# Search and choice of the sample queries' keys spread over 128 partitions, in two halves of each 32-partition group

## What is computed

```python
def indexer_topk(qi, wi, ki, q_pos, topk):
    s = einsum('bqhd,bld->bqhl', qi, ki) * IDX_DIM ** -0.5
    score = einsum('bqhl,bqh->bql', relu(s), wi) * N_IDX_HEADS ** -0.5
    score = where(key_pos <= q_pos, score, -inf)
    _, idx = top_k(score, topk)
...
q, k, v, qi, ki, wi, u = mixer_inputs(hs, pos_s, norm_mix_pre, w_in)      # 64 sample queries
ki_all = concatenate([cache_kidx[page_table], ki])                         # 4096 past + 8 new keys each
idx, valid = indexer_topk(qi, wi, ki_all, pos_s, 256)
a_o = sparse_attend(q, gathered keys, gathered values, valid)
y_ssm, hr, hi = s5_scan(...);  s_o = glu_out(y_ssm, w_glu, b_glu)
hs = residual_block(hs, a_o, s_o, w_out, ..., w_up, w_down, ...)           # the same for the prompt
```

## Time and profile before

| | before |
|---|---|
| median of 3 runs | 3765.61 us |
| lowest and highest run | 3762.29 and 3767.79 us |
| span of the profiled execution, first to last instruction | 3765.1 us |
| mean granted TensorE clock | 0.902 |
| busy share PE, DVE, ACT, POOL | 81%, 57%, 49%, 34% |

### The profile page before, as it was taken

One profiled execution on the slowest core, in us unless ns is written; L12 is line 12 of the kernel. 1 busy time (PEld: TensorE's weight loads), 2 busy tenths in 40 slices (PEclk: granted clock), 3 DMA queues, 4 the chain that ended last, 5 costly groups with the idle time before them and its releaser, 6 DMA issues.

```text
span 3765.1 us, 47305 instructions
## 1 busy us (share of the span) xinstructions
PE 3068.1 (81%) x15388; PEld 2414.3 (64%) x15388; DVE 2160.7 (57%) x4196; ACT 1845.4 (49%) x3065; POOL 1286.6 (34%) x1134
## 2 busy tenths in 40 slices
PE   7997535537778889997788999868888999789997
PEld 6886421214556668765577886546677888678885
DVE  4433952973356984467897443777995443643333
ACT  3322413722446755575674556756754554433333
POOL 1333510313013561252265114522663112235454
PEclk9998767767779999998899999989999999989998
DMA  4444344527332232123223112242222111522222
GB/s 153 141 138 166 64 153 108 135 68 222 99 113 76 81 94 68 55 78 136 97 77 95 54 43 63 81 148 69 72 90 83 54 40 50 177 81 87 79 79 76
DMA packets 201425, 361.56 MB, mean 96 GB/s; under 512 B 56202, under 2 KB 113612, under 8 KB 199740
## 3 DMA queue, kind: packets, MB, share of 16 engines
q1 hardware_dynamic: 182652, 332.01, 27.9%
q0 software_dynamic: 9312, 18.14, 1.5%
q10 hardware_dynamic: 9216, 8.39, 0.7%
HBM read 298.64 MB, written 67.01 MB: 97 GB/s over the span
## 4 chain that ended last, share of the span: by engine, by line
PE 42%; DVE 18%; issue 12%; ACT 5%; POOL 4%; DMA 2%; SPq 1%; ACTq 1%; POOLq 0%; DVEq 0%
PE r L1532 11%; PE r L1564 9%; PE po L1612 4%; PE r L1505 3%; PE tr L1603 3%; DVE junk_v_b L2242 3%; POOL acc_b L2008 2%; ACT junk_a_b L1873 2%; DVE trial_b L2194 2%; DVE up_b L2089 2%; DVE dn_b L2089 2%; PE sc L1580 1%; PE sc L1591 1%; PE sc L1590 1%; PE r L1675 1%
## 5 line engine op out<-in xcount | busy, mean ns | idle before, releaser
L1564 PE MATMUL r<-dn_b,h_b 128*128 128x512 f32 x2880 | 727.0, 408 | 111.8 <-DVE dn_b L2089 51.2
L1564 PEld LDWEIGHTS r<-dn_b,h_b 128*128 128x128 f32 x2880 | 551.4, 196 | 273.1 <-DVE dn_b L2089 61.7
L2008 POOL TENSOR_TENSOR acc_b<-acc_b,part_b 128x512 f32<-128x512 f32 x375 | 527.8, 1427 | 517.2 <-ACT part_b L1824 516.3
L1532 PE MATMUL r<-x_hi_b,up_b 128*128 128x512 f32 x2048 | 660.2, 396 | 7.6 <-DVE x_lo_b L2108 4.2
L1532 PEld LDWEIGHTS r<-x_hi_b,up_b 128*128 128x128 f32 x2048 | 389.2, 190 | 105.5 <-issue 13.0
L1873 ACT ACTIVATE junk_a_b<-score_b,trial_b 128x384 int8<-128x384 f32 (+13 forms) x266 | 347.4, 1306 | 148.5 <-DVE trial_b L2194 147.8
L1989 POOL TENSOR_TENSOR hr_b<-hr_b 128x512 f32<-128x512 f32 x128 | 153.5, 1199 | 738.4 <-ACT hr_b L1811 738.1
L1532 PE MATMUL r<-x_lo_b,up_b 128*128 128x512 f32 x1024 | 402.7, 393 | 0.0
L1824 ACT ACTIVATE part_b<-r 128x512 f32<-128x512 f32 x390 | 223.9, 594 | 225.0 <-PE r L1564 156.0
L1612 PEld LDWEIGHTS po<-V_sb,pT_b 128*128 128x128 f32 x2176 | 291.5, 195 | 23.2 <-issue 3.1
L1900 ACT ACTIVATE pT_b<-tr 128x512 f32<-128x512 f32 (+3 forms) x320 | 169.0, 528 | 259.5 <-PE tr L1603 257.8
(11 more groups left out here) (385 smaller groups left out, 5696.3 us busy)
## 6 DMA issues: line engine op xcount, KB each, us to landing
raw_b<-w_up SPq DMA_DIRECT2D x128, 512.0 KB, 3.8
raw_b<-w_down SPq DMA_DIRECT2D x128, 512.0 KB, 3.5
raw_b<-w_out SPq DMA_DIRECT2D x64, 256.0 KB, 3.2
kv_b<-kv_pages SPq DMA_DIRECT2D x96, 128.0 KB, 4.0
kv_b<-kv_pages POOLq DMA_DIRECT2D x96, 128.0 KB, 3.8
x_tok_sb<-x_all SPq DMA_DIRECT2D x17, 512.0 KB, 4.5
xT_sb<-xT_all SPq DMA_DIRECT2D x17, 512.0 KB, 4.8
kic<-kidx_d SPq DMA_DIRECT2D x4, 2048.0 KB, 8.5
```

The lines of the kernel that those rows point to most:

```text
L1532: mm = pe.matmul(x[:], wt[:, c], y[:, k], start=k == n == 0, stop=(k, n) == (KD - 1, 2))
L1564: mm = pe.matmul(x[:], f[:, tok], w[:, col], start=c == n == 0, stop=(c, n) == (KQ - 1, 2))
L2008: pool.tensor_tensor(dst, dst, part[:, add_no[key] % 2, :], ALU.add).then_inc(add_pool, 1)
```

## The change

The 64 queries no longer stand in 64 partitions with 4104 keys each. Each 32-partition group holds 16 queries twice: its first 16 partitions with the first 2048 past keys, its last 16 with the other 2048. Both have 8 columns for the new keys, 2056 in all; in the first half these are masked off.

The sums over the heads go to 128 rows (`wsel` has a zero-filled form for each half), two chunks of keys are accumulated in one bank, and one copy takes both. ScalarE counts columns 0 to 1095, VectorE 1096 to 2055. Wherever a count, or the number of ties in the other half, is needed, a `stream_shuffle` swaps the two halves of each group and an add joins them. `rep` gets one form for each half, so that one matmul of 128 rows by 128 columns takes the place of two of 64 by 64. The loads of `newmask` and `rep32` become 16 loads on POOL's queue.

```diff
-    CUT = 2064
+    HK = PAST // 2 + DECT
+    CUT = 1096
...
-        sjunk_a, sjunk = place_at("sjunk_a", [NS, CUT], BF16), place_at("sjunk", [NS, NK], BF16)
+        sjunk_a, sjunk = place_at("sjunk_a", [P, CUT], BF16), place_at("sjunk", [P, HK], BF16)
...
-                sp.dma_start(newmask[:], A["newmask"]).then_inc(ss_ld, 16)
...
-                sp.dma_start(rep32[:], A["rep"]).then_inc(ss_ld, 16)
...
-                        wait(pe, wt_ok, w)
+                        s = w % 2 if w < NC else 1
+                        wait(pe, wt_ok, w // 2 if w % 2 == 0 else 0)
                         for k in range(2):
-                            mm = pe.matmul(ring[2][0:NS, 0:m], wsel[:, k, :], rl[:, (2 * w + k) % 4, 0:m], start=k == 0, stop=k == 1)
+                            mm = pe.matmul(ring[2][:, 0:m], wsel[:, s, k, :], rl[:, (2 * w + k) % 4, 0:m],
+                                           start=k == 0 and w % 2 == 0, stop=k == 1 and s == 1)
...
-                    for b in range(2):
-                        mm = pe.matmul(x[64 * b:64 * b + 64, 0:m], rep[:, 2 * r + b, :], stie[:, c * KC:c * KC + m], start=False, stop=True)
-                    mm.then_inc(ss_full, 1)
+                    s = c // (NC // 2) if c < NC else 1
+                    at_ = c * KC - s * PAST // 2
+                    pe.matmul(x[:, 0:m], rep[:, s, 2 * r:2 * r + 2, :].rearrange("p b n -> p (b n)"), stie[:, at_:at_ + m],
+                              start=False, stop=True).then_inc(ss_full, 1)
...
+                    if u[0] == "SQ":
+                        for a in range(4):
+                            for z in range(2):
+                                rows, q = slice(32 * a + 16 * z, 32 * a + 16 * z + 16), slice(16 * a, 16 * a + 16)
+                                pool.dma_start(newmask[rows], A["newmask"][q]).then_inc(half_ld, 16)
+                                pool.dma_start(rep32[rows], A["rep"][q]).then_inc(half_ld, 16)
...
-                        pool.tensor_copy(rep[:], rep32[:]).then_inc(sprep, 1)
...
+                other_half = [*range(16, 32), *range(16)]
+
+                def whole(x, partner):
+
+                    c.step(dve.stream_shuffle(partner, x, other_half))
+                    c.step(dve.tensor_tensor(x, x, partner, ALU.add))
...
+                        whole(sboth[:, 0:1], sboth[:, 1:2])
...
-                    c.step(dve.tensor_scalar(sjunk[:, CUT:NK], smask[:, CUT:NK], strial[:].bitcast(F32), 0.0, ALU.is_ge, ALU.add,
+                    c.step(dve.tensor_scalar(sjunk[:, CUT:HK], smask[:, CUT:HK], strial[:].bitcast(F32), 0.0, ALU.is_ge, ALU.add,
...
                         c.step(dve.tensor_scalar(j, s, z(1), 0.0, ALU.is_ge, ALU.add, accum_out=z(2)))
+                        whole(z(2), z(6))
...
                         c.step(dve.tensor_scalar(e, s, z(3), 0.0, ALU.is_gt, ALU.add, accum_out=z(4)))
+                        whole(z(4), z(6))
...
+                        for n in range(2):
+                            c.up(dve.tensor_scalar(rep[:, n], rep32[:], second[:, n:n + 1], None, ALU.mult))
...
                         c.step(dve.tensor_tensor_scan(s, e, e, 0.0, ALU.add, ALU.bypass))
+                        c.step(dve.stream_shuffle(z(6), smask[:, HK - 1:HK], other_half))
+                        c.step(dve.tensor_tensor(z(6), z(6), second[:, 1:2], ALU.mult))
+                        c.step(dve.tensor_tensor(z(5), z(5), z(6), ALU.subtract))
...
-                        for k in range(2):
-                            dve.tensor_scalar(wsel[:, k, :], sel[:, k, :], wcol[:, k:k + 1], None, ALU.mult).then_inc(wsel_ok, 1)
+                        dve.memset(wsel[:], 0.0).then_inc(wsel_ok, 1)
+                        by_half = ident[:].rearrange("p (a z q) -> p z a q", a=4, z=2)
+                        c.step(dve.tensor_reduce(quads[:], by_half[:, 1], AX.X, ALU.add))
+                        c.step(dve.tensor_reduce(second[:, 1:2], quads[:], AX.X, ALU.add))
+                        c.step(dve.tensor_scalar(second[:, 0:1], second[:, 1:2], -1.0, 1.0, ALU.mult, ALU.add))
...
+                        for n in range(2):
+                            for k in range(2):
+                                dve.tensor_scalar(wsel[:, n, k].rearrange("p (a z q) -> p z a q", a=4, z=2)[:, n],
+                                                  sel[:, k].rearrange("p (a q) -> p a q", a=4), wcol[:, k:k + 1], None,
+                                                  ALU.mult).then_inc(wsel_ok, 1)
...
-                            dve.tensor_copy(smask[:, at_:at_ + m], ring[2][0:NS, 0:m]).then_inc(wt_ok, 1)
...
+                        elif w % 2:
+                            dve.wait_ge(wt_full, w + 1)
+                            dve.tensor_copy(smask[:, w // 2 * KC:w // 2 * KC + KC], ring[2][:, 0:KC]).then_inc(wt_ok, 1)
```

More of the change, by code:

```diff
@@ L1121, in blend @@
         at[0] = after_kv
-        smask = place_at("smask", [NS, NK], size=0)
+        smask = place_at("smask", [P, HK], size=0)
         sprob = place_at("sprob", [P, NK])
-        stie = place_at("stie", [NS, NK], BF16)
+        stie = place_at("stie", [P, HK], BF16)
         pTs = place_at("pTs", [P, 3, 4, P])
-        strial, sturn = place_at("strial", [NS, 1], I32), place_at("sturn", [NS, 1], I32)
-        scount, sboth, sbest = place_at("scount", [NS, 2]), place_at("sboth", [NS, 1]), place_at("sbest", [NS, 6])
+        strial, sturn = place_at("strial", [P, 1], I32), place_at("sturn", [P, 1], I32)
+        scount, sboth, sbest = place_at("scount", [P, 2]), place_at("sboth", [P, 2]), place_at("sbest", [P, 8])
+        second, quads = place_at("second", [P, 2]), place_at("quads", [P, 4])
         qid = place_at("qid", [NS, NIH, 2, HD])
         qiS = place_at("qiS", [P, DECB, NIH, DECT])
-        wcol, sel, wsel = place_at("wcol", [P, 2]), place_at("sel", [P, 2, NS]), place_at("wsel", [P, 2, NS])
-        newmask = place_at("newmask", [NS, DECT])
+        wcol, sel, wsel = place_at("wcol", [P, 2]), place_at("sel", [P, 2, NS]), place_at("wsel", [P, 2, 2, P])
+        newmask = place_at("newmask", [P, DECT])
         spt = place_at("spt", [1, DECB * NPAGE], I32)
         q16, qz = place_at("q16", [P, 4, P]), place_at("qz", [P, DECB, NKV, QPK, DECT])
-        rep32, rep = place_at("rep32", [NS, DECB, NS]), place_at("rep", [NS, DECB, NS], BF16)
+        rep32, rep = place_at("rep32", [P, DECB, NS]), place_at("rep", [P, 2, DECB, NS], BF16)
         vn = place_at("vn", [DECT, DECB, P])
@@ L1666, in sample_scores @@
                         pe.wait_ge(gate_ok, N_GATE)
-                        pe.wait_ge(sprep, 5)
+                        pe.wait_ge(sprep, 4)
                         pe.wait_ge(smask_ok, 1)
@@ L2059, in sample_part @@
                         pool.memset(aTs[:], 0.0).then_inc(sprep, 1)
[L2060 to L2062 removed]
+                        pool.wait_ge(ss_ld, 16 * (3 + DECB))
+                        pool.wait_ge(sprep, 2)
                         for n in range(NKV):
@@ L2294, in sample_search @@
                         dve.wait_ge(scount_ok, n)
-                        c.step(dve.scalar_tensor_tensor(out=sboth[:], in0=scount[:, 1:2], scalar=2.0, in1=scount[:, 0:1],
+                        c.step(dve.scalar_tensor_tensor(out=sboth[:, 0:1], in0=scount[:, 1:2], scalar=2.0, in1=scount[:, 0:1],
                                                         op0=ALU.mult, op1=ALU.subtract))
+                        whole(sboth[:, 0:1], sboth[:, 1:2])
                         back = -1.0 if b == BITS - 1 else float(2 ** b)
-                        c.step(dve.tensor_scalar(sturn[:], sboth[:], float(2 * TOPK - CUT), back, ALU.is_lt, ALU.mult))
+                        c.step(dve.tensor_scalar(sturn[:], sboth[:, 0:1], float(2 * TOPK - 2 * CUT), back, ALU.is_lt, ALU.mult))
                         if b == 0:
@@ L2341, in sample_part @@
                     elif u[0] == "SI" and 0 <= u[1] - 1 <= NC:
                         w = u[1] - 1
-                        m = KC if w < NC else DECT
-                        at_ = ((w % 2) * NC // 2 + w // 2) * KC if w < NC else PAST
-                        dve.wait_ge(wt_full, w + 1)
-                        if w < NC:
-                            dve.tensor_copy(smask[:, at_:at_ + m], ring[2][0:NS, 0:m]).then_inc(wt_ok, 1)
-                        else:
-                            dve.tensor_tensor(smask[:, at_:at_ + m], ring[2][0:NS, 0:m], newmask[:], ALU.add).then_inc(wt_ok, 1)
+                        if w == NC:
+                            dve.wait_ge(half_ld, 16 * 16)
+                            c.step(dve.tensor_scalar(quads[:, 0:1], second[:, 0:1], NEG, None, ALU.mult))
+                            c.step(dve.tensor_scalar(newmask[:], newmask[:], quads[:, 0:1], None, ALU.add))
+                            dve.wait_ge(wt_full, NC + 1)
+                            dve.tensor_tensor(smask[:, PAST // 2:HK], ring[2][:, 0:DECT], newmask[:], ALU.add).then_inc(wt_ok, 1)
+                        elif w % 2:
```

(2 more changed lines are left out.)

12 lines of the change are left out of this document (6 added, 6 removed).

## The result

The changed kernel takes 3731.36 us (median of 4 runs, 3730.24 to 3733.96) against 3766.70 us before (4 runs): ratio 0.9903, 95% interval 0.9891 to 0.9915. The profiled execution took 3730.24 us, with a span of 3728.6 us instead of 3765.1. On another chip the same kernel gave 3726.34 against 3773.32 us, 0.9882 [0.9865, 0.9898]. Two executions far outside all others, one of run 7 (4585 us) and one of the kernel before beside it (7054 us), are left out of what follows. The forecast was 3736.8 us: right in sign and inside its range, but 5.4 us above the measured median. Against the span it had summed 28.8 us of gain, and 36.5 us came.

A forecast was written before the change was run, and what follows sets the result against it. VectorE bounds the kernel from the late gates to the end of the choice. Gains of 0.2 + 3.3 + 10.0 + 12.3 + 3.0 = 28.8 us off the 3765.1 span, plus half a microsecond, gave 3736.8 us; range 3727 to 3750.

The forecast's parts named there:

- Start and SI: Work before gate 0: the start loses 0.4 us, SI gains 0.6, so gate 0 comes 0.2 us earlier.
- 128 weights instead of 64 cost nothing: In SI, the matmuls keep their 512 moving columns, so the wider weights add no time.
- POOL's issues cost nothing: At the start, POOL's 16 loads take 17.8 us and end near 565, before its next work at 573.09.
- Gates: Gates 9 to 15 speed up from 4.07 us each towards TensorE's 3.43, gaining 3.3 us.
- the choice between the ends: For gates 9 to 15, 3.3 us was taken from a range of 1.2 to 4.5 us gained.
- the collision: In gates 9 to 15, GpSimd's product holds up VectorE's settle, 3.9 us a gate, cutting the gain to 1.2 us.
- Counts and settles: Counts 16 to 31: shorter counts gain 18.0 us, exchanges cost 7.6, waits for ScalarE 0.4; 10.0 us gained.
- The slower rival: Each shuffle's load of lanes costs 1.28 us, like ScalarE's table load: 12 us slower, 3777.5 us; chance 0.04.
- Choice: Counts, marks, scan and last operations shrink from 4104 to 2056 columns, gaining 12.3 us (11.3 to 13).
- SS: The mask matmul saves time in 27 units of the first three rounds: 3 us gained, between 0 and 4.3.
- one bf16 matmul should be one such pass: 0.12 us less: In each SS unit, the single mask matmul takes one 0.214 us pass instead of 0.33 us for two.
- Rivals: Gates unchanged, exchanges dearer: 3744.6 us, 0.15; POOL slow: 3748, 0.07; lanes dear: 3777.5, 0.04; lost behind choice: 3765.6, 0.04.

The follow-up runs named there:

- run 7: Kernel before with one more count over 2040 columns ahead of the choice's first count; 3765.89 us, ratio 0.9991.
- run 8: Changed kernel with the 16 loads of newmask and rep32 issued by SP instead of POOL; 3735.11 us against 3726.34 for the changed kernel.
- run 2: Changed kernel with each exchange of the bits and of the choice's two counts done twice; 3747.63 us, ratio 0.9929.
- run 1: Changed kernel without the exchanges in the bits and the choice's two counts, each half searched by its own counts; 3723.50 us, ratio 0.9876.
- runs 3 and 9: Changed kernel with the mask added by two matmuls of 128 rows and 64 columns, 3730.47 us; changed kernel without any mask matmul, 3720.30 us.
- run 6: Changed kernel with the mask added by two matmuls of 64 rows and 64 columns, as in the kernel before; 3728.88 us, ratio 0.9908.
- run 4: Changed kernel with twelve more counts over 2056 columns before the choice's first count, 29 us late; 3759.85 us, ratio 0.9976.

## Why the prediction was right, and where it was not

*Start and SI* (forecast 0.2, measured 0.3): right in the sum by two errors that cancel. The start was to lose 0.4 us and gained 0.6 (the first bit of the prompt at 572.29 instead of 572.87): the first score came 1.6 us earlier, where I took 0.7, and `wsel` cost 1.0 on the path, where I took 1.1. SI was to gain 0.6 and lost 0.2: the 0.63 us of waiting before the last full chunk's sum went, but the step "128 weights instead of 64 cost nothing" failed, since a sum over the heads takes 1.98 us instead of 1.93 in each full chunk, and the last short one 0.58 instead of 0.37. That POOL's issues cost nothing held (0.49 us each; done at 556, forecast 565), and that SP's two issues count held (run 8).

*Gates* (3.3, measured 4.5): the floor. The step that missed is the choice between the ends: I let the collision begin behind some slack. It never set the pace: an operation held for 0.4 us in one bit of three fell among waits for ScalarE of 0.65 to 0.84 us. My bit had GpSimd's product end 3.24 us after a count starts; at 678 it ended 2.4 us after (679.00, count at 676.58), since the sigmoid stands ahead of ScalarE's next count and not behind it. Run 2 shows how near it is: 0.39 us a bit more brings it back, and then a single add is held for 1.06 us. The rule that I had set against the trace (the Trainium skill, SBUF — State Buffer, "Who interferes with whom": a VectorE operation with two SBUF inputs and a GpSimd one that reads SBUF exclude each other for a whole instruction) would have made this part 1.2 us. The trace agrees with the rule by the held adds, 1.06 us in run 2 and 0.31 at 710.60 in the changed kernel (which ends with GpSimd's product at 710.91), but its price came only with run 2's longer bits.

*Counts and settles* (10.0, measured 12.1): right in mechanism, mis-sized in its terms. The load of lanes is 0.01 us instead of 0.10 and the shuffle 0.15: an exchange costs 0.38 to 0.39 instead of 0.47 (run 1), 1.4 us over 16. VectorE's wait for ScalarE is 0.18 us in a bit without S unit, where I had 0.09. And behind gate 15 the settle of the prompt's bit (L2203, L2194 before) is no longer held in most bits (0.16 us at 717.20, where it has 0.34 at 726.12 in the kernel before), which I hadn't counted. On the instruction for the lanes (the Trainium skill, Vector Engine (DVE) Microarchitecture Reference, "The reshape front-end and per-opcode configuration") the trace agrees: it stands ahead of each shuffle, as LOAD_MASK_SELECT. The slower rival hung on its price and falls at 0.01 us.

*Choice* (12.3, measured 12.7): right, term by term (2.35, 1.28, 4.44 us).

*SS* (3.0, measured 8.2): wrong. The step "one bf16 matmul should be one such pass: 0.12 us less" failed: two 64-column matmuls run side by side and cost what one costs, and both shapes, 64 rows or 128 columns, pay for a change of tiling (runs 3 and 9). What was gained there instead goes with granted clock: 4.1 us by the shape of the mask's matmuls (run 6); most of the other 4.1 us in the first and third stretch (2.2 and 1.7 between the two sets of rows), which go in part with where the stage falls (2.7 us lost in run 4, 1.8 gained in run 7) and in part with something that no run isolated. I had written that the last round and what follows gains nothing; 4.6 us were gained in those two stretches.

*Rivals.* None came true. The gates left their old rate and the exchanges were cheaper than forecast, POOL's loads were done 16 us before its next work, and the lanes cost 0.01 us. The gain was not lost behind the choice: 6.9 us more came than stood at the first SS matmul. Of the 7.7 us by which the sum fell short of the span, 5.2 lie in the SS rounds; there the mechanism was wrong, and that a gain came at all in that part is luck.

## What to carry to other kernels

Rows that fill half of the partitions can be split into halves of their columns. An exchange of one number between partitions of a group costs 0.38 us by shuffle and add, a third of the 1.1 us saved in a count of 2040 columns, so the longer the rows, the more of the half is kept. Where one engine's steps are about as long as those of another that it shares time with, price the next small addition with the holds that it brings (0.93 us where 0.39 were added), not with its own length. Between matmuls of 64-column tiles keep the tiles' shape even for a matmul that could use all 128 columns: the pair cost 0.25 us a unit less than the single one (runs 3 and 9), though VectorE let only 2.9 of 6.8 us through here.
